# Lowest levels of a block inverse: from doubling on TensorE in the scans to 16x16 substitution on VectorE in the projections

## The reference

```
z = xn @ w_in                       # r, k, v, low-rank parts, convolution, gates
# for each direction d:
decay = exp(-exp(w_log));  a = sigmoid(...);  kd = k * (1 + (a - 1) * k_a)
# scan over tokens, one 64x64 state S per head:
sa = S a_t                          # a_t = -kk, b_t = kk * a
S  = S * w_t + sa b_t^T + v_t k_t^T
y_t = S r_t
```

## Time and profile before

| | |
|---|---|
| runs | 3045.55 us median, 3035.25 to 3046.99 |
| profiled execution | 3056.41 us, span 3054.6 us |
| TensorE (PE) busy | 2895.7 us, 95% |
| VectorE (DVE) busy | 1448.7 us, 47% |
| ScalarE (ACT) busy | 845.1 us, 28% |
| GpSimd (POOL) busy | 923.9 us, 30% |
| chain that ended last | PE 90%, DMA 4%, issue 2%, DVE 2% |

### The profile page before, as it was taken

How to read it: one execution, slowest core, us unless ns; L and a number is a source line. 1 busy time by engine, 2 the same in 40 slices (tenths; PEclk the granted TensorE clock), 3 DMA queues, 4 the chain that set the end, 5 groups by cost and what they waited for, 6 DMA issues and landing times.

```text
span 3054.6 us, 71870 instructions
## 1 busy us (share of the span) xinstructions
PE 2895.7 (95%) x30862; PEld 2676.2 (88%) x30862; DVE 1448.7 (47%) x2610; ACT 845.1 (28%) x1639; POOL 923.9 (30%) x1296
## 2 busy tenths in 40 slices
PE   4899999999999799999999997999799999999997
PEld 2799999999999577777777777999799999999997
DVE  1363554455356256666666664253443333333333
ACT  3434334324333133333333332111321111111111
POOL 0321111111111266666666663222121121112111
PEclk7999999999999799999999999999899999999999
DMA  7131441442343323333333335222111111111111
GB/s 287 39 110 64 146 124 58 146 131 80 116 146 97 101 82 90 99 103 96 92 98 106 105 111 196 83 78 71 45 42 42 42 41 41 41 41 41 41 34 62
DMA packets 195566, 272.36 MB, mean 89 GB/s; under 512 B 15840, under 2 KB 137056, under 8 KB 195168
## 3 DMA queue, kind: packets, MB, share of 16 engines
q1 hardware_dynamic: 186336, 232.73, 25.5%
q0 software_dynamic: 7200, 28.84, 2.5%
q10 hardware_dynamic: 1760, 6.82, 0.6%
HBM read 192.31 MB, written 76.02 MB: 88 GB/s over the span
## 4 chain that ended last, share of the span: by engine, by line
PE 90%; DMA 4%; issue 2%; DVE 2%; SPq 1%; ACT 1%; POOL 0%; DVEq 0%; POOLq 0%; ACTq 0%
PE inv L664 24%; PE gbank L664 24%; PE bank L664 22%; PE ser L664 16%; PE inv L841 2%; DMA ring<-in_wblocks 2%; PE gbank L815 1%; DMA vb<-v_d 1%; DVE xr L1511 0%; DMA xt_d<-xt_s 0%; DVE xb L1887 0%; SPq L481 0%; POOL wsp L627 0%; DVE xt L1665 0%; DVE gmat L1644 0%
## 5 line engine op out<-in xcount | busy, mean ns | idle before, releaser
L627 POOL TENSOR_TENSOR wsp<-ring,wsp 128x1024 fp32r<-128x1024 f32 x88 | 215.4, 2448 | 853.4 <-ACT wsp L1389 834.1
L552 POOL TENSOR_TENSOR wsp<-ring,wsp 128x1024 fp32r<-128x1024 f32 x67 | 170.2, 2541 | 728.4 <-ACT wsp L1191 728.4
L664 PE MATMUL gbank<-xn_hi,wsp 128*128 128x384 f32 x1312 | 349.4, 340 | 18.2 <-DVE xn_lo L1844 18.2
L664 PE MATMUL bank<-xn_hi,wsp 128*128 128x384 f32 x1312 | 346.6, 338 | 0.4 <-POOL wsp L627 0.4
L664 PE MATMUL inv<-xn_hi,wsp 128*128 128x384 f32 x1312 | 344.8, 338 | 0.0
L664 PEld LDWEIGHTS gbank<-xn_hi,wsp 128*128 128x128 f32 x1312 | 239.5, 188 | 22.7 <-issue 14.9
L664 PEld LDWEIGHTS bank<-xn_hi,wsp 128*128 128x128 f32 x1312 | 238.3, 188 | 2.3 <-POOL wsp L627 0.7
L664 PEld LDWEIGHTS inv<-xn_hi,wsp 128*128 128x128 f32 x1312 | 237.9, 187 | 1.6 <-POOL wsp L552 1.1
L584 POOL TENSOR_TENSOR xtb<-xt,trim 128x256 f32<-128x256 f32 (+1 forms) x219 | 145.5, 665 | 290.7 <-DVE xt L1665 286.2
L1389 ACT ACTIVATE wsp<-ring 128x1024 fp32r<-128x1024 f32 x88 | 92.6, 1053 | 472.1 <-PE inv L664 393.0
L664 PE MATMUL ser<-xn_hi,wsp 128*128 128x384 f32 x816 | 217.3, 340 | 5.4 <-DVE xr L1511 5.4
(11 more groups left out here) (362 smaller groups left out, 5921.9 us busy)
## 6 DMA issues: line engine op xcount, KB each, us to landing
ring<-in_wblocks SPq DMA_DIRECT2D x195, 512.0 KB, 3.6
ub<-op_d SPq DMA_DIRECT2D x144, 256.0 KB, 2.6
op_d<-ar SPq DMA_DIRECT2D x32, 576.0 KB, 5.4
op_d<-bk SPq DMA_DIRECT2D x32, 576.0 KB, 6.2
vb<-v_d SPq DMA_DIRECT2D x144, 64.0 KB, 2.6
xt_d<-xt_s POOLq DMA_DIRECT2D x8, 576.0 KB, 3.3
v_d<-vn SPq DMA_DIRECT2D x8, 576.0 KB, 7.0
xb_d<-cv SPq DMA_DIRECT2D x8, 576.0 KB, 3.3
```

The source lines that it names most:

```text
L552: GT(wsp[s % 2][1][:], ring[(N_ADA_RING + s) % RING][:], wsp[s % 2][0][:].bitcast(F32), ALU.subtract).then_inc(S["wsplit_lo"], 1)
L627: nc.gpsimd.tensor_tensor(wsp[b % 2][1][:], ring[(N_MIX0 + b) % RING][:], wsp[b % 2][0][:].bitcast(F32), ALU.subtract).then_inc(S["wl_ok"], 1)
L664: return nc.tensor.matmul(out, lhsT, rhs, start=start, stop=stop)
```

## The change

The inverse starts three levels higher (`FIRST = 3`): a unit enters the scans with its 16x16 diagonal blocks already inverted, and goes through three levels, one unit in each round instead of two. The blocks are made in the projection loop:

- TensorE's `diagonal(p)`, between the fills cb and za, computes the 64x64 diagonal blocks of the coupling matrix again from the operands: 72 products of 64x64x64 for each pair, in 6 fills. ScalarE copies them to `kt` and `rt`, whose contents are no longer needed.
- SyncE writes both to DRAM (`g_d`), waits for that, and reads the 16x16 blocks back in 32 DMAs (`blocks_in`) so that 72 partitions hold one block each, of every head and direction.
- VectorE's `substitution(p - 1)` inverts them by 15 steps of forward and backward substitution: 60 small TENSOR_TENSOR and 2 copies. It stands in the next pair's work between `keys(p, 0)` and the wait for `ks`. The last pair's is spread over 15 steps of the scans, one step of substitution ahead of each.
- SyncE writes the inverted blocks to DRAM in 16 DMAs (`inverse_out`) into `x_d`, which 8 DMAs have filled with zeros at the start of the projections. `unit_in` loads a unit's 64 KB of it straight into `xt`, as one DMA more.

The unit's grams and transposes are made one step later than before (s + 2 and s + 3 in place of s + 3 and s + 4), the loop starts at s = -3, `token_major` uses bank 3, and some buffers shrink or grow.

```
+FIRST = 3
+SUB = 16
+Q = HD // SUB
+BLK = 2 * Q * (T // C)
-AFTER = ["k", "r", "v", "ks", "cc", "ch", "vt", "cb", "za", "bon", "zb"]
+AFTER = ["k", "r", "v", "ks", "cc", "ch", "vt", "cb", "g", "za", "bon", "zb"]
+DIAGONAL = [(f"g{h}", cg) for cg in range(G) for h in range(2)]
-SETS = 5
+SETS = 4
-TOKS = 4
+TOKS = 3
         def at_level(s, i):
-            both = [(v, lev) for v, lev in ((s + 2, i), (s + 1, 3 + i)) if 0 <= v < UNITS]
-            return sorted(both, key=lambda x: x[0] % 2)
+            return [(s + 1, FIRST + i)] if 0 <= s + 1 < UNITS else []
@@ SyncE
+            def blocks_in(p):
+                for b in range(2):
+                    for q in range(Q):
+                        part, rows, cs = block_rows(b, q)
+                        for h in range(2):
+                            for d in range(2):
+                                sp.dma_start(sub_a(p)[part, d, h, :, :], g_d[p, h, rows, :, d, cs].rearrange("r j s -> j r s")).then_inc(S["blk_in"], 16)
+            def inverse_out(p):
+                if p == 0:
+                    sp.wait_ge(S["zero_out"], 16 * PAIRS)
+                sp.wait_ge(S["inv_ok"], p + 1)
+                for b in range(2):
+                    for q in range(Q):
+                        part, rows, cs = block_rows(b, q)
+                        for h in range(2):
+                            sp.dma_start(x_d[p, :, rows, h, cs], sub_y(p)[part, h, :, :]).then_inc(S["x_out"], 16)
+            for p in range(PAIRS):
+                sp.dma_start(x_d[p].rearrange("j p h t -> p j (h t)"), zero[:].unsqueeze(1).to_broadcast([P, NC, 2 * HD])).then_inc(S["zero_out"], 16)
                     if name == "cc":
+                        if p:
+                            inverse_out(p - 1)
                     if name == "za":
+                        emptied(p, "g1")
+                        for h in range(2):
+                            sp.dma_start(g_d[p, h].rearrange("p j d t -> p (j d t)"), (kt, rt)[h][:]).then_inc(S["g_out"], 16)
+                        sp.wait_ge(S["g_out"], 32 * (p + 1))
+                        blocks_in(p)
@@ unit_in
+                sp.dma_start(xt[:, q, :, :], x_d[p, j]).then_inc(u_in[q], 16)
-                        sp.wait_ge(u_in[q], 64 * (v // LOADS) + 32 * (d + 1))
+                        sp.wait_ge(u_in[q], 80 * (v // LOADS) + 32 * (d + 1) + 16)
@@ TensorE
+            def diagonal(p):
+                pe.wait_ge(S["op_ok"], 8 * p + 7)
+                for cg in range(G):
+                    o = [free_bank(p, f"g{h}", cg) for h in range(2)]
+                    for i in range(G):
+                        for d in range(2):
+                            c, at = chunk(d, G * cg + i), slice((2 * i + d) * HD, (2 * i + d + 1) * HD)
+                            for h in range(2):
+                                hs = halves_of[h]
+                                for b in halves_of:
+                                    x = slice(c * C + b.start, c * C + b.stop)
+                                    last = mm(o[h][b, at], bk0[d][hs, x], ar0[d][hs, x], True, True)
+                                if (i, d) == (G - 1, 1):
+                                    last.then_inc(S["fill_full"], 1)
-            def first_turn(v):
-
-                pe.wait_ge(S["m1_ok"], v + 1)
...
-                for h in range(2):
-                    for b in halves_of:
-                        ins = mm(banks[3][b, h * HD:(h + 1) * HD], m1t[v % 2][b, h, :], ident[b, b], True, True)
@@ ScalarE
                 empty(p, "v", lambda cg: vf[:, cols(cg)], ACT.Copy)
+                if p:
+                    act.wait_ge(S["inv_ok"], p)
                 empty(p, "ks", lambda cg: kk[:, cols(cg)], ACT.Sqrt)
+                act.wait_ge(S["prod_ok"], p + 1)
+                for name, cg in DIAGONAL:
+                    act.wait_ge(S["fill_full"], FL.full(p, name, cg))
+                    A((kt, rt)[int(name[1])][:, cols(cg)], banks[FL.bank(p, name, cg)][:, :GN], ACT.Copy).then_inc(ev["A"], 1)
@@ VectorE
+            def substitution(p, some=range(SUB - 1)):
+                a, y = sub_a(p), sub_y(p)
+                if 0 in some:
+                    dve.wait_ge(S["blk_in"], 16 * 8 * Q * (p + 1))
+...
+                    for d in range(2):
+                        ch.step(V.tensor_copy(y[:, d, :, :], eye[0:BLK, :, :]))
+                for x in some:
+                    spans = ((slice(0, SUB - 1 - x), SUB - 1 - x, slice(SUB - 1 - x, SUB)), (slice(x + 1, SUB), x, slice(0, x + 1)))
+                    n, m = SUB - 1 - x, x + 1
+                    for d, (rows, row, cs) in enumerate(spans):
+                        settled(done[1] if x == 0 else done[d])
+                        ch.step(V.tensor_tensor(sub_tmp(p, d, n, m), a[:, d, :, rows, row].unsqueeze(3).to_broadcast([BLK, 2, n, m]),
+                                                y[:, :, row, cs].unsqueeze(2).to_broadcast([BLK, 2, n, m]), mul))
+                    for d, (rows, row, cs) in enumerate(spans):
+                        ins = V.tensor_tensor(y[:, :, rows, cs], sub_tmp(p, d, n, m), y[:, :, rows, cs], add)
-            def first_sum(v):
-                dve.wait_ge(S["x0_full"], v + 1)
-                V.tensor_tensor(xt[:, place_of(v), :, :], heads(banks[3][:, 0:P]), two(i64[:]), add).then_inc(S["xt0_ok"], 1)
```

More of the change, by code:

```diff
@@ L393, in levels_of @@
         def levels_of(both):
[L394 to L397, removed]
+            return pick([lev - FIRST for v, lev in both])
         def a3(x):
@@ L596, in _ @@
             pool.wait_ge(S["zero_ok"], 1)
-            for s in range(-4, UNITS):
+            for s in range(-3, UNITS):
                 for i in range(3):
@@ L836, in turn @@
                     pe.wait_ge(S["tt_ok"], s + 1)
-                if i == 0 and there(s + 2):
-                    pe.wait_ge(S["xt0_ok"], s + 3)
                 for v, lev in both:
@@ L1023, in _ @@
                     if i == 0:
-                        if there(s + 3):
-                            gram(s + 3, 1, (0, 1, 2))
+                        if there(s + 2):
+                            gram(s + 2, 1, (0, 1, 2))
                         if there(s):
@@ L1029, in _ @@
                         y_state(s)
-                    if i == 2:
-                        if there(s + 4):
-                            gram(s + 4, 0, (2,))
-                        if there(s + 3):
-                            first_turn(s + 3)
+                    if i == 2 and there(s + 3):
+                        gram(s + 3, 0, (2,))
                     if inverses:
@@ L1045, in _ @@
                         right(s, i)
-                    if i == 0 and there(s + 3):
-                        token_major(s + 3)
+                    if i == 0 and there(s + 2):
+                        token_major(s + 2)
                     if i == 1:
@@ L1050, in _ @@
                             mean(*x)
-                        if there(s + 4):
-                            gram(s + 4, 0, (0, 1))
+                        if there(s + 3):
+                            gram(s + 3, 0, (0, 1))
                     if i == 2:
@@ L1357, in _ @@
                             y_out(s - 1)
-                    if i == 1 and there(s + 3):
-                        tokens(s + 3)
+                    if i == 1 and there(s + 2):
+                        tokens(s + 2)
                     if at_level(s, i):
@@ L1587, in _ @@
                 keys(p, 0)
+                if p:
+                    substitution(p - 1)
                 filled(p, "ks")
@@ L1739, in _ @@
             first_state(0)
-            for s in range(-4, UNITS):
+            for s in range(-3, UNITS):
                 p, j = divmod(s, NC)
+                if NC <= s < NC + SUB - 1:
+                    substitution(PAIRS - 1, [s - NC])
                 for i in range(3):
@@ L1753, in _ @@
                         y_add(s - 1)
-                    if i == 0 and there(s + 3):
-                        gram(s + 3, 1)
+                    if i == 0 and there(s + 2):
+                        gram(s + 2, 1)
                     if i == 1:
@@ L1763, in _ @@
                             centred(*x)
[L1764 to L1765 removed]
                         if there(s + 3):
[L1767 removed]
+                            gram(s + 3, 0)
                     if at_level(s, i):
@@ L1901, in blocks @@
         return np.concatenate([m[b:b + HD, b:b + HD] for b in (0, HD)])
-    for lev in range(LEVELS):
+    for lev in range(FIRST, LEVELS):
         n = 2 << lev
```

145 lines of the change are left out of this document (84 added, 61 removed).

## The result

Over six runs of each, the kernel before takes 3038.3 us (median, 3035.25 to 3046.99) and the changed one 3012.14 us (3009.03 to 3022.16). The ratio is 0.9908, with a 95% interval of 0.9892 to 0.9924: 28 us faster by the ratio (26 by the medians), where 62.5 were forecast and 2980 us named. In the two profiled executions it is 3056.41 against 3011.74 us, 44.7 less.

A forecast was written before the change was run, and what follows sets the result against it. TensorE bounds the projections; TensorE's work and a ring of waits bound the scans. -99 + 13 + 4 - 9 + 28 - 1.5 + 2 = -62.5 us from 3056.41: 2994 profiled, 2980 named; 80% range 2935 to 3050.

The forecast's parts named there:

- the length of SyncE's iteration with a weight block: In the scans: 10.1 us before, 10.5 with the new DMA, against a new step of 9.35.
- the term +13: In the scans: late bonus tiles hold `scaled` in the last two of four iterations, 1.9 us a pair, +13 us.
- SyncE holds the scans: Rival: in the scans all four iterations are late and landings slower, 53 us instead of 13, total 3020; chance 0.07.
- the ring: In the scans: waits among engines bound round 2, TensorE's work rounds 0 and 1; step 9.35 us, -99 us.
- the way into the scans: Before step 0: the first ramp step and levels 0 to 2 of unit 0 go; -9 us.
- `token_major` behind `mrow`: In the scans: waits once a pair for ScalarE's copy of the modulation row, about half a us; +4 us.
- `diagonal`: In the projections: 144 records a pair on TensorE's path, 3.5 us a pair, +28 us.
- Substitution and blocks at nothing: In the projections: substitution fits VectorE's 22.7 us idle time and blocks land by 591, in time; cost 0.
- The slower rival: In the projections: 64 B DMAs land each for itself, delaying 25 us a pair, 175 in all, 3155; chance 0.10.
- a little late: Rival: in the projections blocks or substitution come up to 6 us late, up to +37, near 3005; chance 0.16.
- The zeros and the mask: In the prologue: zeros run beside TensorE's first fills, a smaller mask tile saves perhaps 1.5 us; -1.5 us.
- Throughput decides: Rival: in the scans TensorE's work alone bounds, 1.94 us less a step, -140, total 2925; chance 0.12.

The follow-up runs named there:

- r1: e3_both with the four token transposes of a unit done twice on TensorE; 2974.54 us, ratio 0.9776 to the kernel before.
- e3_both: Changed kernel with the bonus tile issued two iterations earlier and SyncE no longer waiting in the scans for weight blocks to land; 2959.47 us, ratio 0.9701.
- l1: e3_both with SyncE waiting for the 32 DMAs of blocks to land ahead of the issue of `ga_d`; 2947.79 us, one run.
- b3_both: The kernel before with the same two SyncE edits as e3_both; 3047.03 us, ratio 0.9989.
- r2: e3_both with VectorE's mask of the transpose done twice in all three rounds; 3015.07 us, ratio 0.9902 to the kernel before.

## Why the prediction was wrong

- **The step that failed** is the length of SyncE's iteration with a weight block, taken as 10.1 us and with the new DMA 10.5, and from it the term +13. It was read from one iteration, a quick one. From bonus tile to bonus tile over a weight block at j = 4 to 6 the changed kernel takes 12.0 us in the mean of 18 (10.5 to 13.9); the kernel before took 11.7, waits for a step's end among them, against a step of 10.7. So each iteration loses near 3 us on a step, not 1.15, and the steps j = 6 to 8 wait, three where the forecast had the last two of four. The term is 62 us (728.9 less 666.5), not 13: 36 as waits, some 24 as clock, which this term did not have at all. The place was right: `scaled` waits for `fbon` at the end of the four iterations. This is the rival "SyncE holds the scans" (53 us for this term, 3020), to which I gave 0.07. That its time lies within 8 us of the measured one is in part chance: it had 1.65 us lost an iteration and no clock.
- **The tally, profile against profile without the last term**: 29.5 us won where 62.5 were forecast, 33 short. SyncE's term is 49 of it; the ring (10 more than forecast) and the way into the scans (6 more) gave a third of that back.
- **The ring** was right: light step 9.13 to 9.14 for 9.35. Round 0 came out at 3.24, near step 70 (3.21), not at 3.45: r1 shows that its floor is TensorE's, but I had priced what stands beside the inverse 0.21 too high. e3_both has 103 us less than before in steps 0 to 70; forecast without SyncE's term, -99 + 4 + 2 for 72.
- **`token_major` behind `mrow`**: +4 forecast, 4.8 measured in 8 waits.
- **The way into the scans**: -10.3 with the last pair's `diagonal` in it (2.5, and a stall of 2.05 in it), so near -15; forecast -9.
- **`diagonal`**: +28 forecast. The group is 2.26 us (0.25 for 16 records, not 0.39), the block it stands in grows from 12.81 to 15.27: 2.46 a pair. Six pairs grew by 20.0, 3.3 each: 2.46, stalls of 0.84 and 1.44 us in the last two, and about 0.5 a pair that nothing here explains (GpSimd's splits, one for each weight block, follow each other at 12.57 us where it was 12.48). With the first pair (3.1) and the last it is near 28: right in size, in part by luck, since the group was priced too high and the stalls and the 0.5 not at all.
- **Substitution and blocks at nothing**: right. 12.9 us (13 forecast), and the blocks land at about 586 in l1, not 591 to 613. The slower rival fell with it, and "a little late" too. The Trainium skill (DMA: Bandwidth & Descriptors, Specifications) gives 512 B as the least transfer for line rate; here 4608 runs of 64 B landed at the pace at which their DMAs were issued, so it cost nothing that l1 shows.
- **The zeros and the mask**: -1.5 forecast for the prologue. At `kk` of pair 0, ahead of the first `diagonal`, the changed kernel is 1.7 us earlier (187.15 to 185.47); but b3_both, with the prologue of before, is there at 184.48, so this is within what executions differ by.
- **Throughput decides** (2925) fell: r2 shows the ring bounding two rounds.

## What to carry to other kernels

When a change shortens a loop, list every engine and queue that has a loop of its own over the same steps, and compare its mean iteration, over many, with the new step; SyncE's here were 1.0 us above the old step already and lived off the light steps between. A queue that waits for each landing has a length of its own, and an early tile that is issued behind such waits is the first to be late. The share of waits for the compute engines in the DMA queue (163 us before, 55 after) is its slack, and can be read before the change.

## What the hardware showed that was not expected

- After TensorE's waits of 2 to 4 us the granted clock was lower, and over the scans it made the same records 24 us longer. It is 0.50 over 1155 to 1160 of the changed kernel, the lower of its two levels (1.2 GHz), and 1.00 (2.4 GHz) in e3_both from 1080 to 1740. A light step, steps 52 (from its second round) and 53 of the changed kernel (columns as in the windows above):

```profile
1551.50:1560.60 9.10, 9.10 (x209) 7.30 (x207) 5.78 (x16) 3.36 (x11) 4.66 (x11) 1.00 0.36 105
1622.70:1630.60 7.90, 5.66 (x112) 4.41 (x110) 3.10 (x8) 2.27 (x7) 4.50 (x11) 1.00 0.44 125
1630.70:1643.20 12.50, 10.00 (x185) 7.88 (x183) 6.10 (x17) 3.20 (x10) 4.48 (x11) 0.86 0.38 113
```
- A burst of 144 short products (64x64x64, 288 records) with the DMA engines 91 to 98% busy before it stands still for 3.4 to 4.2 us in four of the eight pairs and for 1.1 to 2.1 in the others, with no wait for another engine; the three long pairs among the six above are 5 to 7 us longer than the records make them. One block later, with the DMA engines 1 to 3% busy in the burst, it still stands for 0.7 to 1.3; 72 products (144 records) there do not stand at all. All these stalls end 2.2 to 2.7 us after a transfer of 16 KB of instructions began.
- 32 DMAs of 9 KB in runs of 64 B land 13.5 us after the first issue.
